# Fast-matrix feed-forward on one core: sums made in place of bank copies, loads issued by ScalarE

## The chip, the cores and the metric

The kernel runs on one core of one Trainium2 chip. The core has a matrix engine (TensorE, PE in the profile; its weight loads are PEld), VectorE (DVE), ScalarE (ACT), GpSimd (POOL) and SyncE (SP), which here only issues transfers. Each engine runs its own list of instructions in order, and the lists meet only through semaphores. A DMA is put into a queue by the engine that issues it, and 16 DMA engines carry it out. The metric is the device time of one execution in microseconds.

## The reference, cut to what matters

One encoder layer on 560 tokens (16 meta rows, 512 prompt frames, 32 frames of a running stream), width 2048, in float32:

```
xn   = RMSNorm(h);  P = xn @ w_in                      # q, k, v, gates, conv input
mix  = [stick-breaking attention heads | short gated conv groups], normed per group
h    = h + RMSNorm(mix @ w_out)
xf   = RMSNorm(h)
ff   = silu(xf @ w_gate) * (xf @ w_up)                 # D_FF = 5632
h    = h + RMSNorm(ff @ w_down)                        # the output; keys, values and conv rows go out too
```

The change touches only the feed-forward part, the last three lines, for the 544 tokens that are not meta rows.

## The kernel before, in words

Each float32 product is made of three: both operands are split into a rounded part and a rest (hi, lo), and hi*hi, hi*lo and lo*hi are summed in a PSUM bank. The feed-forward products use a scheme with 7 block products instead of 8: tokens are two halves of 272 (TH), inputs two halves of 8 blocks of 128 (KH), outputs two columns of 128. The seven products of a step are called B11, B21, T2, T3, T1, T4, B22, in this order; each is 24 matmuls of 128x128 by 272 columns. B11, B21 and B22 take a block of the weights as it is, T1 to T4 take combinations that VectorE makes (`combine`). The token side needs seven combinations too (A11, A12, S2, S3, S1, A22, S4).

There are 44 gate/up steps (even: gate, odd: up; a pair yields 256 columns of ff) and then 24 down steps (`DSTEPS`, in 6 blocks of 4 steps; a block takes 4, 4, 4, 4, 3, 3 pairs of ff, and its 4 steps cover the 2048 outputs). Step 43 is `LAST`, step 44 is the first down step (d = 0).

What each engine does in a step, in the order of its list:

- SyncE (L613 and on) loads the weights of the next step as two panels of 1 MB: `load_panel(step, 0)` once the seven tiles of the step before last are split, `load_panel(step, 1)` once tile T1 of the step before is split. Between the two stands, for even steps, `store_hidden`: it waits for `hid_split` and stores the seven combinations of a pair of ff (hid_hi and hid_lo, each 128 x 7 x 272 float32) to device memory. During the down steps its list also holds `load_hidden`, which brings a combination of a block of ff back into one of 12 slots (`xd`), two DMAs each. SyncE's queue is one list, so a wait for one transfer holds all behind it.
- ScalarE rounds each of the seven tiles (`tile_high`, L1336; tile i waits until product i-4 is done, as the ring has four places), copies bank snapshots after B11, T2 and T3 to m1, u2 and m7 (`copy_out`, L1369), applies silu to the quarters of the gate, and rounds the seven ff combinations (`round_hidden`, L1375).
- VectorE subtracts for each tile the rest (`tile_rest`, L1711), makes the combinations of the next step's weights (`combine`, L1725; T2 needs the second panel), adds bank and snapshot (`c11` L1778, `c22` L1784, `c21` L1789) into `gate` in gate steps and into `hid` in up steps, multiplies in place (`times_gate`, `times_gate_rest`), makes the four sums of ff (`hidden_sums`, in the gate step after) and the rest of the seven (`hidden_rest`, L1815, in the next up step), and in the down steps adds banks to y (`take_down`, L1874 and L1876).
- TensorE waits per product for its split tile and for the bank that it overwrites: B22 of a gate step for `c22_made`, T2 for `m1_copied`, T1 for `u2_copied`, T4 for `m7_copied`; in the down steps T2 waits for `take_down(B11)` of the same step.

The order of work is written out by hand; no planner sets it.

Of the kernel before, what the change touches and what calls it, by code (L numbers as in the profile page):

```python
# [25 lines left out]
P = 128  # L26
# [3 lines left out]
def build_layer(nc, x_prompt, x_sample, cache_k, cache_v, state_conv, meta, w_in, w_out, conv_w,  # L30
# [90 lines left out]
    with ExitStack() as ctx:  # L121
# [63 lines left out]
        m1 = sb_at("m1", 134144, [P, TH])  # L185
        u2 = sb_at("u2", 135232, [P, TH])
        m7 = sb_at("m7", 169984, [P, TH])
        t_hi = sb_at("t_hi", 137216, [P, RING_T, KH * P], F32R)
        t_lo = sb_at("t_lo", 153600, [P, RING_T, KH * P], F32R)
# [311 lines left out]
        def _(sp):  # L501
# [99 lines left out]
            def load_hidden(i):  # L601

                b, q = i // 7, i % 7
                sp.wait_ge(hid_stored, 32 * first_pair[b + 1])
                for part in range(2):
                    sp.dma_start(xd[:, i % XD, part, 0:KBS[b], :].bitcast(F32),  # L606
                                 ff_scr[part][:, HID_OF[q], first_pair[b]:first_pair[b + 1], :])\
                      .then_inc(xd_loaded[i % XD], 16)

            def load_hidden_after(step, q):  # L610

                if step == LAST and q < 6:
                    sp.wait_ge(product_done, 7 * step + q + 1)  # L613
                    load_hidden(2 * q)
                    load_hidden(2 * q + 1)
                elif step >= STEPS and (step - STEPS) % NQ == NQ - 1:
                    i = (step - STEPS) // NQ * 7 + q + XD
                    if i < 7 * len(KBS):
                        sp.wait_ge(product_done, 7 * step + q + 1)
                        load_hidden(i)  # L620

            for step in range(1, ALL):
                if step == 2:
                    sp.wait_ge(xs_lo, 8)
                if step > 2:
                    sp.wait_ge(tile_lo, 7 * (step - 1))
                if step == 1:
                    sp.wait_ge(tile_lo, T1 + 1)
                load_panel(step, 0)
                if step >= LAST + 2:  # L630
                    for q in range(4, 7):
                        load_hidden_after(step - 2, q)
# [421 lines left out]
        def _(act):  # L1054
# [310 lines left out]
            def copy_out(out, step, q, letter, made, free):  # L1365
                act.wait_ge(product_done, 7 * step + q + 1)
                if step:
                    act.wait_ge(free, step)
                A(out[:, :], step_bank(step, letter), ACT.Copy).then_inc(made, 1)  # L1369

            def round_hidden(j):
                act.wait_ge(hid_summed, 4 * (j + 1))
                if j:
                    act.wait_ge(hid_stored, 32 * j)
                nc.scalar.copy(hid_hi[:, :, :], hid[:, :, :]).then_inc(hid_rounded, 1)  # L1375

            for step in range(STEPS):
# [7 lines left out]
                copy_out(m1, step, B11, "a", m1_copied, c11_made)  # L1385
# [12 lines left out]
                tile_high(ahead)  # L1398
                tile_high(ahead + 1)
# [41 lines left out]
        def _(dve):  # L1441
# [326 lines left out]
            def quarters(step):  # L1768
                return hid if step % 2 else gate

            def c11(step):
# [4 lines left out]
                if step >= 3 and step % 2:  # L1776
                    dve.wait_ge(hid_stored, 32 * (step // 2))
                V.tensor_tensor(quarter(quarters(step), 0, 0), step_bank(step, "c"), m1[:, :], ALU.add)\  # L1778
                    .then_inc(c11_made, 1)

            def c22(step):
                dve.wait_ge(product_done, 7 * step + T1 + 1)
                dve.wait_ge(m7_copied, step + 1)
                V.tensor_tensor(quarter(quarters(step), 1, 1), step_bank(step, "a"), m7[:, :], ALU.add)                    .then_inc(c22_made, 1)  # L1784

            def c21(step):
                dve.wait_ge(product_done, 7 * step + T4 + 1)
                dve.wait_ge(u2_copied, step + 1)
                V.tensor_tensor(quarter(quarters(step), 1, 0), step_bank(step, "b"), u2[:, :], ALU.add)                    .then_inc(c21_made, 1)  # L1789

            def times_gate(step):
# [3 lines left out]
                V.tensor_tensor(quarter(hid, 0, 1), step_bank(step, "a"), quarter(gate, 0, 1), ALU.mult)                    .then_inc(c12_up, 1)  # L1795

            def times_gate_rest(step):
                dve.wait_ge(c21_made, step + 1)
                V.tensor_tensor(hid[:, 0:2, :], hid[:, 0:2, :], gate[:, 0:2, :], ALU.mult)
                V.tensor_tensor(hid[:, 3, :], hid[:, 3, :], gate[:, 3, :], ALU.mult).then_inc(hid_made, 1)  # L1800

            def hidden_sums(j):

                d21, d11, d12, d22, s1, s2, s4 = (hid[:, h, :] for h in range(7))
# [3 lines left out]
                V.tensor_tensor(d21, d11, d21, ALU.subtract).then_inc(hid_summed, 1)  # L1808
                V.tensor_tensor(s2, s1, d11, ALU.subtract).then_inc(hid_summed, 1)
# [8 lines left out]
            for step in range(STEPS):  # L1818
# [59 lines left out]
            for d in range(DSTEPS):  # L1878
# [9 lines left out]
                if d == 1:  # L1888
                    hidden_rest(FF // 2 - 1)
# [8 lines left out]
                if d == 0:  # L1898
                    hidden_sums(FF // 2 - 1)
# [125 lines left out]
```

## Time and profile before

| quantity | value |
|---|---|
| median of 3 runs | 2493.34 us (2493.3 to 2494.7) |
| the profiled execution: its own time | 2493.23 us |
| its span, first to last instruction | 2491.5 us, mean granted clock 0.981 |
| gate/up steps | from 972.2 to 1960.8 us |
| down steps | from 1960.8 to 2449 us |
| VectorE busy in the span | 1553.6 us |
| ScalarE busy in the span | 1009.2 us |

The span leaves 1.7 us outside. Busy time of TensorE counts a matmul from start to modelled end. A row of a timeline gives start and duration; in brackets stands how long the engine had been idle and what ended it.

### The profile page before, as it was taken

What the parts mean: (1) busy time and instruction counts of PE and PEld (TensorE: products, weight loads), DVE (VectorE), ACT (ScalarE), POOL (GpSimd) and SP (SyncE); (2) the same over time, 40 slices, a digit from 0 to 9 for tenths busy, and PEclk for the clock granted to TensorE, in tenths of its full rate; (3) what the DMA queues carried; (4) which work ended last, traced back from release to release, by engine and by line L of the source; (5) the groups of instructions that cost most, each with busy time, mean ns of one, the idle gap of its engine ahead of it and who ended that gap; (6) DMA issues with size and microseconds to landing.
All of it is one profiled execution on the core that took longest, in us unless ns stands there. A gap on an engine that the chain in (4) does not pass through costs nothing.

```text
span 2491.5 us, 42064 instructions
## 1 busy us (share of the span) xinstructions
PE 2382.3 (96%) x18188; PEld 2329.9 (94%) x18188; DVE 1553.6 (62%) x1755; ACT 1009.2 (41%) x1257; POOL 103.7 (4%) x155
## 2 busy tenths in 40 slices
PE   8999999999999994899999999999999889999996
PEld 7999999999999993899999999999999889999995
DVE  5324333343443228777777777777777678888896
ACT  6344444433333214544444444444444333333344
POOL 0000000000011110000000000000000000000024
PEclk9999999999999997899999999999999999999997
DMA  7222322232225321334454443445444845663552
GB/s 236 85 66 82 90 76 73 82 89 83 83 73 168 86 85 72 102 127 155 134 165 134 138 143 124 157 134 165 133 144 138 307 153 203 224 201 102 195 188 72
DMA packets 332636, 327.92 MB, mean 132 GB/s; under 512 B 8700, under 2 KB 291220, under 8 KB 332324
## 3 DMA queue, kind: packets, MB, share of 16 engines
q1 hardware_dynamic: 318080, 318.47, 40.0%
q10 hardware_dynamic: 14372, 6.77, 0.9%
q8 instruction: 144, 2.36, 0.4%
q14 instruction: 40, 0.33, 0.0%
HBM read 264.20 MB, written 61.00 MB: 131 GB/s over the span
## 4 chain that ended last, share of the span: by engine, by line
PE 80%; DVE 10%; issue 4%; ACT 4%; DMA 2%; SPq 1%; POOL 0%; POOLq 0%; ACTq 0%; DVEq 0%
PE ps L427 30%; PE ps L975 28%; PE ps L1032 17%; PE ps L742 4%; ACT t_hi L1336 2%; DVE t_lo L1711 2%; DVE panel L1725 2%; SPq L606 1%; DMA panel<-in_w_down_dram 1%; DMA ff_lo_scr<-hid_lo 1%; PE ps L686 1%; DVE xs L1733 1%; DVE misc L1737 0%; DVE y_left L1925 0%; DVE wide L1701 0%
## 5 line engine op out<-in xcount | busy, mean ns | idle before, releaser
L975 PE MATMUL ps<-xs,t_hi 128*128 128x272 f32 x4928 | 943.3, 291 | 51.0 <-DVE xs L1733 19.1
L975 PEld LDWEIGHTS ps<-xs,t_hi 128*128 128x128 f32 x4928 | 780.7, 190 | 57.2 <-issue 54.7
L975 PE MATMUL ps<-xs,t_lo 128*128 128x272 f32 x2464 | 716.6, 291 | 0.0
L1711 DVE TENSOR_TENSOR t_lo<-panel,t_hi 128x1024 fp32r<-128x1024 f32 (+1 forms) x405 | 485.9, 1200 | 195.1 <-ACT t_hi L1336 187.2
L1336 ACT CAST t_hi<-panel 128x1024 fp32r<-128x1024 f32 (+1 forms) x405 | 411.9, 1022 | 470.5 <-PE ps L1032 230.6
L1032 PE MATMUL ps<-xd,t_hi 128*128 128x272 f32 x2464 | 470.3, 290 | 16.9 <-DVE t_lo L1711 8.6
L975 PEld LDWEIGHTS ps<-xs,t_lo 128*128 128x128 f32 x2464 | 467.3, 190 | 0.0
L427 PE MATMUL ps<-act_hi,w_hi 128*128 128x272 f32 (+1 forms) x2048 | 435.6, 294 | 3.2 <-DVE act_lo L1548 2.1
L427 PE MATMUL ps<-act_lo,w_hi 128*128 128x272 f32 (+1 forms) x2048 | 427.0, 290 | 0.0
L427 PE MATMUL ps<-act_hi,w_lo 128*128 128x272 f32 (+1 forms) x2048 | 427.0, 290 | 0.0
L1032 PEld LDWEIGHTS ps<-xd,t_hi 128*128 128x128 f32 x2464 | 390.4, 190 | 18.7 <-issue 9.6
L1032 PE MATMUL ps<-xd,t_lo 128*128 128x272 f32 x1232 | 358.1, 291 | 0.0
L427 PEld LDWEIGHTS ps<-act_hi,w_hi 128*128 128x128 f32 x2048 | 323.0, 189 | 7.3 <-DVE act_lo L1548 2.5
L427 PEld LDWEIGHTS ps<-act_hi,w_lo 128*128 128x128 f32 x2048 | 324.3, 189 | 0.0
L427 PEld LDWEIGHTS ps<-act_lo,w_hi 128*128 128x128 f32 x2048 | 324.0, 189 | 0.0
L413 DVE TENSOR_TENSOR w_lo<-w_raw,w_hi 128x1024 fp32r<-128x1024 f32 x126 | 158.4, 1258 | 195.9 <-ACT w_hi L407 195.1
L407 ACT CAST w_hi<-w_raw 128x1024 fp32r<-128x1024 f32 x128 | 133.7, 1046 | 282.7 <-PE ps L427 222.5
L1032 PEld LDWEIGHTS ps<-xd,t_lo 128*128 128x128 f32 x1232 | 233.5, 190 | 0.0
L1336 ACT CAST t_hi<-t_raw 128x1024 fp32r<-128x1024 f32 (+1 forms) x68 | 69.8, 1026 | 64.1 <-PE ps L1032 35.7
L1725 DVE TENSOR_TENSOR t_raw<-panel,panel 128x1024 f32<-128x1024 f32 (+1 forms) x67 | 79.4, 1185 | 22.2 <-DMA panel<-in_w_down_dram 17.3
L1369 ACT ACTIVATE m<-ps 128x272 f32<-128x272 f32 x88 | 35.0, 398 | 142.2 <-PE ps L975 142.2
L1482 DVE TENSOR_TENSOR misc<-misc 128x1440 f32<-128x1440 f32 x8 | 13.3, 1658 | 114.3 <-ACT misc L1119 114.3
(176 smaller groups left out, 1746.0 us busy)
## 6 DMA issues: line engine op xcount, KB each, us to landing
w_raw<-in_w_in_dram SPq DMA_DIRECT2D x96, 512.0 KB, 3.9
panel<-in_w_up_dram SPq DMA_DIRECT2D x44, 1024.0 KB, 5.5
panel<-in_w_gate_dram SPq DMA_DIRECT2D x43, 1024.0 KB, 6.8
panel<-in_w_down_dram SPq DMA_DIRECT2D x32, 1024.0 KB, 6.5
ff_hi_scr<-hid_hi SPq DMA_DIRECT2D x22, 952.0 KB, 4.5
ff_lo_scr<-hid_lo SPq DMA_DIRECT2D x22, 952.0 KB, 7.6
w_raw<-in_w_out_dram SPq DMA_DIRECT2D x32, 512.0 KB, 4.1
xd<-ff_hi_scr SPq DMA_DIRECT2D x28, 544.0 KB, 9.4
```

The source lines that it names most:

```text
L407: nc.scalar.copy(w_hi[:, k % SLOTS, :], raw_slot(k)).then_inc(hi_ready, 1)
L413: engine.tensor_tensor(w_lo[:, k % SLOTS, :], raw_slot(k), w_hi[:, k % SLOTS, :].bitcast(F32), ALU.subtract).then_inc(lo_ready, 1)
L427: mm = nc.tensor.matmul(out[:, h, :], w[:, k, col:col + width], x[:, x_at + k, token + h * half:token + (h + 1) * half], start=begins, sto ...
L606: sp.dma_start(xd[:, i % XD, part, 0:KBS[b], :].bitcast(F32), ff_scr[part][:, HID_OF[q], first_pair[b]:first_pair[b + 1], :])\
L686: return nc.tensor.transpose(out, src, ident[0:n, 0:n])
L742: return nc.tensor.matmul(out, w, x, start=start, stop=True, skip_group_check=True)
L975: mm = nc.tensor.matmul(out, w[:, k, :], xs[:, x, part, k, :], start=begins and k == 0 and w is hi and part == 0, stop=k == KH - 1 and w i ...
L1032: mm = nc.tensor.matmul(out[:, n, :], w[:, k, n * P:(n + 1) * P], xd[:, slot, part, k, :], start=q in (B11, B21, T3) and k == 0 and w is h ...
L1336: nc.scalar.copy(tile_of(t_hi, i), raw_tile(i)).then_inc(tile_hi, 1)
L1369: A(out[:, :], step_bank(step, letter), ACT.Copy).then_inc(made, 1)
L1711: V.tensor_tensor(tile_of(t_lo, i), raw_tile(i), tile_of(t_hi, i).bitcast(F32), ALU.subtract)\
L1725: V.tensor_tensor(out, x, y, ALU.subtract).then_inc(t_made, 1)
```

## The change

The in-place results of the up step go: m1, u2 and m7 get a second buffer each, used in odd (up) steps, and c11, c22, c21 of an up step sum into them. The product with the gate then reads the buffer and the gate and writes `hid`. Around it the order of ff's sums, rounding and rest changes, and the loads of ff's combinations move from SyncE's list to ScalarE's; loads 7 to 11 of the start move from step 43/44 to step 45.

```diff
-        m1 = sb_at("m1", 134144, [P, TH])
-        u2 = sb_at("u2", 135232, [P, TH])
-        m7 = sb_at("m7", 169984, [P, TH])
+        m1, u2, m7 = ([sb_at(f"{name}_{odd}", (at, at_odd)[odd], [P, TH]) for odd in range(2)]
+                      for name, at, at_odd in (("m1", 134144, 171264), ("u2", 135232, 209024), ("m7", 170176, 136320)))
...
SyncE:
-                if step >= LAST + 2:
-                    for q in range(4, 7):
-                        load_hidden_after(step - 2, q)
                 if step > 3 and step % 2 == 0 and step // 2 - 2 < FF // 2:
                     store_hidden(step // 2 - 2)
-                if step >= LAST + 1:
-                    for q in range(2):
-                        load_hidden_after(step - 1, q)
...
-                if step >= LAST + 1:
-                    for q in range(2, 4):
-                        load_hidden_after(step - 1, q)
ScalarE:
-            def copy_out(out, step, q, letter, made, free):
+            def copy_out(out, step, q, letter, made):
                 act.wait_ge(product_done, 7 * step + q + 1)
-                if step:
-                    act.wait_ge(free, step)
-                A(out[:, :], step_bank(step, letter), ACT.Copy).then_inc(made, 1)
+                if step >= 2:
+                    if step % 2:
+                        act.wait_ge(hid_made, step // 2)
+                    else:
+                        act.wait_ge({B11: c11_made, T2: c21_made, T3: c22_made}[q], step - 1)
+                A(out[step % 2][:, :], step_bank(step, letter), ACT.Copy).then_inc(made, 1)
...
+            def load_hidden_after(step, q):
+                first = []
+                if step == LAST:
+                    first = {0: (0, 1), 1: (2, 3), 2: (4, 5), 3: (6,)}.get(q, ())
+                elif step == STEPS + 1 and 0 <= q < 5:
+                    first = (7 + q,)
+                for i in first:
+                    act.wait_ge(product_done, 7 * LAST + i // 2 + 1)
+                    load_hidden(i)
+                d = step - STEPS
+                if d >= 0 and d % NQ == NQ - 1 and 0 <= q < 7:
+                    i = d // NQ * 7 + q + XD
+                    if i < 7 * len(KBS):
+                        act.wait_ge(product_done, 7 * step + q + 1)
+                        load_hidden(i)
...
+                load_hidden_after(step, 0)
                 tile_high(7 * step + 5)
-                copy_out(u2, step, T2, "a", u2_copied, c21_made)
+                load_hidden_after(step, 1)
+                if not is_gate and j:
+                    round_hidden(j - 1)
+                copy_out(u2, step, T2, "a", u2_copied)
                 tile_high(7 * step + 6)
+                load_hidden_after(step, 2)
...
-                copy_out(m7, step, T3, "b", m7_copied, c22_made)
-                if is_gate and step:
-                    round_hidden(j - 1)
+                copy_out(m7, step, T3, "b", m7_copied)
                 tile_high(ahead)
+                load_hidden_after(step, 3)
...
-                    if d == 0 and q == 6:
+                    if d == 1 and q == 4:
                         round_hidden(FF // 2 - 1)
+                    if q == 3:
+                        load_hidden_after(STEPS + d - 1, 6)
+                    else:
+                        load_hidden_after(STEPS + d, q - 4)
VectorE:
+            def sum_of(step, up, t, n):
+                return up[1][:, :] if step % 2 else quarter(gate, t, n)
...
-                if step >= 3 and step % 2:
-                    dve.wait_ge(hid_stored, 32 * (step // 2))
-                V.tensor_tensor(quarter(quarters(step), 0, 0), step_bank(step, "c"), m1[:, :], ALU.add)\
+                V.tensor_tensor(sum_of(step, m1, 0, 0), step_bank(step, "c"), m1[step % 2][:, :], ALU.add)\
...
             def times_gate(step):
+                if step > 1:
+                    dve.wait_ge(hid_stored, 32 * (step // 2))
...
-                V.tensor_tensor(hid[:, 0:2, :], hid[:, 0:2, :], gate[:, 0:2, :], ALU.mult)
-                V.tensor_tensor(hid[:, 3, :], hid[:, 3, :], gate[:, 3, :], ALU.mult).then_inc(hid_made, 1)
+                V.tensor_tensor(quarter(hid, 0, 0), m1[1][:, :], quarter(gate, 0, 0), ALU.mult)
+                V.tensor_tensor(quarter(hid, 1, 1), m7[1][:, :], quarter(gate, 1, 1), ALU.mult)
+                V.tensor_tensor(quarter(hid, 1, 0), u2[1][:, :], quarter(gate, 1, 0), ALU.mult).then_inc(hid_made, 1)
...
                 if step % 2 and step > 1:
-                    hidden_rest(step // 2 - 1)
+                    hidden_sums(step // 2 - 1)
                 tile_rest(7 * step + 4)
+                if step % 2 and step > 1:
+                    more_hidden_sums(step // 2 - 1)
...
-                elif step % 2 == 0:
+                else:
                     c11(step)
+                if step % 2 and step > 1:
+                    hidden_rest(step // 2 - 1)
                 tile_rest(7 * step + 6)
...
-                if step % 2:
-                    c11(step)
-                if after_up:
-                    hidden_sums(step // 2 - 1)
                 tile_rest(ahead)
...
down steps:
                 if d == 1:
-                    hidden_rest(FF // 2 - 1)
+                    hidden_sums(FF // 2 - 1)
+                    more_hidden_sums(FF // 2 - 1)
...
                 tile_rest(7 * step + 6)
-                if d == 0:
-                    hidden_sums(FF // 2 - 1)
+                if d == 1:
+                    hidden_rest(FF // 2 - 1)
```

`more_hidden_sums` holds the last two of the four sums, `hidden_sums` the first two. `load_hidden` itself is unchanged but for its issuer.

## Rows read from the trace of the kernel before

**Rows 1.** The page, first part: busy time, share of the span, instructions.

```profile
PE 2382.3 (96%) x18188; PEld 2329.9 (94%) x18188; DVE 1553.6 (62%) x1755; ACT 1009.2 (41%) x1257; POOL 103.7 (4%) x155
```

**Rows 2.** Waits of TensorE, 1040 to 1950 us: total, times, longest.

```profile
PE ps L975 <- DVE gate L1784: 18.1, 21, 0.9
PE ps L975 <- DVE hid L1784: 0.8, 4, 0.2
```

**Rows 3.** Waits of TensorE, 1950 to 2400 us.

```profile
PE ps L1032 <- DVE t_lo L1711: 8.6, 2, 7.0
PE ps L1032 <- DVE y_left L1874: 6.6, 2, 5.3
PE ps L1032 <- DVE y_left L1876: 0.9, 1, 0.9
```

**Rows 4.** Timeline of TensorE: start, us, instruction [idle before <-released by].

```profile
1283.70 0.48 PE L975 MATMUL ps<-xs,t_hi 128*128 128x272 f32 x2 [0.86 <-DVE gate L1784]
...
1327.16 0.48 PE L975 MATMUL ps<-xs,t_hi 128*128 128x272 f32 x2 [0.86 <-DVE gate L1784]
...
1971.14 0.82 PE L1032 MATMUL ps<-xd,t_hi 128*128 128x272 f32 x2 [7.01 <-DVE t_lo L1711]
...
1977.23 0.48 PE L1032 MATMUL ps<-xd,t_hi 128*128 128x272 f32 x2 [1.26 <-DVE y_left L1874]
...
2006.90 0.79 PE L1032 MATMUL ps<-xd,t_hi 128*128 128x272 f32 x2 [5.30 <-DVE y_left L1874]
```

**Rows 5.** Timeline of VectorE in one pair of steps, and one later split.

```profile
1290.76 2.14 DVE L1815 TENSOR_TENSOR hid_lo<-hid,hid_hi 128x1904 fp32r<-128x1904 f32 x1
...
1305.35 1.22 DVE L1711 TENSOR_TENSOR t_lo<-panel,t_hi 128x1024 fp32r<-128x1024 f32 x1
...
1326.58 0.43 DVE L1784 TENSOR_TENSOR gate<-ps,m 128x272 f32<-128x272 f32 x1
...
1377.69 2.14 DVE L1815 TENSOR_TENSOR hid_lo<-hid,hid_hi 128x1904 fp32r<-128x1904 f32 x1
```

**Rows 6.** Timeline of ScalarE; the last line from its waits, 1020 to 1950 us.

```profile
1293.05 1.05 ACT L1336 CAST t_hi<-panel 128x1024 fp32r<-128x1024 f32 x1 [1.69 <-PE ps L975]
...
1304.17 1.06 ACT L1336 CAST t_hi<-panel 128x1024 fp32r<-128x1024 f32 x1 [3.73 <-DMA panel<-in_w_gate_dram]
...
1321.54 1.79 ACT L1375 CAST hid_hi<-hid 128x1904 fp32r<-128x1904 f32 x1 [0.86 <-DVE hid L1811]
...
1392.17 1.05 ACT L1336 CAST t_hi<-panel 128x1024 fp32r<-128x1024 f32 x1 [4.80 <-DMA panel<-in_w_gate_dram]
...
ACT t_hi L1336 <- DMA panel<-in_w_gate_dram: 68.6, 17, 5.0
```

**Rows 7.** Timeline of SyncE's issues (start, us of issuing).

```profile
1294.20 1.45 SPq L585 DMA_DIRECT2D panel<-in_w_gate_dram  x1
...
1948.63 1.24 SPq L606 DMA_DIRECT2D xd<-ff_lo_scr  x1
...
2049.22 0.43 SPq L606 DMA_DIRECT2D xd<-ff_lo_scr  x1
```

**Rows 8.** Timeline of VectorE in the first two down steps.

```profile
1968.72 1.23 DVE L1725 TENSOR_TENSOR t_raw<-panel,panel 128x1024 f32<-128x1024 f32 x1 [11.68 <-DMA panel<-in_w_down_dram]
...
1976.37 0.71 DVE L1874 COPY y_left<-ps 128x544 f32<-128x544 f32 x1
...
1995.90 1.22 DVE L1725 TENSOR_TENSOR t_raw<-panel,panel 128x1024 f32<-128x1024 f32 x1 [5.62 <-DMA panel<-in_w_down_dram]
...
2006.04 0.72 DVE L1874 COPY y_left<-ps 128x544 f32<-128x544 f32 x1
```

**Rows 9.** Windows of TensorE: length, busy, granted clock, DMA share, GB/s.

```profile
1296.00:1299.00 3.00, 3.00 (x26) 1.00 1.04 345
1971.00:1976.00 5.00, 4.82 (x24) 0.64 1.02 414
2006.90:2013.00 6.10, 6.10 (x30) 0.57 0.95 307
```

More of the change, by code:

```diff
@@ L184, in build_layer @@
         t2_raw = sb_at("t2_raw", 130048, [P, KH, P])
-        m1 = sb_at("m1", 134144, [P, TH])
-        u2 = sb_at("u2", 135232, [P, TH])
-        m7 = sb_at("m7", 169984, [P, TH])
-        t_hi = sb_at("t_hi", 137216, [P, RING_T, KH * P], F32R)
-        t_lo = sb_at("t_lo", 153600, [P, RING_T, KH * P], F32R)
+        m1, u2, m7 = ([sb_at(f"{name}_{odd}", (at, at_odd)[odd], [P, TH]) for odd in range(2)]
+                      for name, at, at_odd in (("m1", 134144, 171264), ("u2", 135232, 209024), ("m7", 170176, 136320)))
+        t_hi = sb_at("t_hi", 137408, [P, RING_T, KH * P], F32R)
+        t_lo = sb_at("t_lo", 153792, [P, RING_T, KH * P], F32R)
         h2_sq = sb_at("h2_sq", 35840, [P, KC, TL])
@@ L599, in store_hidden @@
                     sp.dma_start(ff_scr[part][:, :, j, :], src[:, :, :].bitcast(F32)).then_inc(hid_stored, 16)
[L601 to L620, printed above, removed]
             for step in range(1, ALL):
@@ L1375, in round_hidden, with load_hidden @@
                 nc.scalar.copy(hid_hi[:, :, :], hid[:, :, :]).then_inc(hid_rounded, 1)
+            def load_hidden(i):
+                b, q = i // 7, i % 7
+                act.wait_ge(hid_stored, 32 * first_pair[b + 1])
+                for part in range(2):
+                    act.dma_start(xd[:, i % XD, part, 0:KBS[b], :].bitcast(F32),
+                                  ff_scr[part][:, HID_OF[q], first_pair[b]:first_pair[b + 1], :])\
+                        .then_inc(xd_loaded[i % XD], 16)
+            def load_hidden_after(step, q):
[13 more added lines that the diff above has]
+                        load_hidden(i)
             for step in range(STEPS):
@@ L1384, in _ @@
                     x_high(S3, 0, 1, s_made, 2)
-                copy_out(m1, step, B11, "a", m1_copied, c11_made)
+                copy_out(m1, step, B11, "a", m1_copied)
                 tile_high(7 * step + 4)
@@ L1765, in _ @@
             x_rest(S2, 5, a11)
-            def quarters(step):
-                return hid if step % 2 else gate
+            def sum_of(step, up, t, n):
+                return up[1][:, :] if step % 2 else quarter(gate, t, n)
             def c11(step):
@@ L1783, in c22 @@
                 dve.wait_ge(m7_copied, step + 1)
-                V.tensor_tensor(quarter(quarters(step), 1, 1), step_bank(step, "a"), m7[:, :], ALU.add)                    .then_inc(c22_made, 1)
+                V.tensor_tensor(sum_of(step, m7, 1, 1), step_bank(step, "a"), m7[step % 2][:, :], ALU.add)\
+                    .then_inc(c22_made, 1)
             def c21(step):
@@ L1788, in c21 @@
                 dve.wait_ge(u2_copied, step + 1)
-                V.tensor_tensor(quarter(quarters(step), 1, 0), step_bank(step, "b"), u2[:, :], ALU.add)                    .then_inc(c21_made, 1)
+                V.tensor_tensor(sum_of(step, u2, 1, 0), step_bank(step, "b"), u2[step % 2][:, :], ALU.add)\
+                    .then_inc(c21_made, 1)
             def times_gate(step):
@@ L1794, in times_gate @@
                 dve.wait_ge(silu_made, 4 * (step // 2 + 1))
-                V.tensor_tensor(quarter(hid, 0, 1), step_bank(step, "a"), quarter(gate, 0, 1), ALU.mult)                    .then_inc(c12_up, 1)
+                if step > 1:
+                    dve.wait_ge(hid_stored, 32 * (step // 2))
+                V.tensor_tensor(quarter(hid, 0, 1), step_bank(step, "a"), quarter(gate, 0, 1), ALU.mult)\
+                    .then_inc(c12_up, 1)
             def times_gate_rest(step):
                 dve.wait_ge(c21_made, step + 1)
-                V.tensor_tensor(hid[:, 0:2, :], hid[:, 0:2, :], gate[:, 0:2, :], ALU.mult)
-                V.tensor_tensor(hid[:, 3, :], hid[:, 3, :], gate[:, 3, :], ALU.mult).then_inc(hid_made, 1)
+                V.tensor_tensor(quarter(hid, 0, 0), m1[1][:, :], quarter(gate, 0, 0), ALU.mult)
+                V.tensor_tensor(quarter(hid, 1, 1), m7[1][:, :], quarter(gate, 1, 1), ALU.mult)
+                V.tensor_tensor(quarter(hid, 1, 0), u2[1][:, :], quarter(gate, 1, 0), ALU.mult).then_inc(hid_made, 1)
+            d21, d11, d12, d22, s1, s2, s4 = (hid[:, h, :] for h in range(7))
             def hidden_sums(j):
-                d21, d11, d12, d22, s1, s2, s4 = (hid[:, h, :] for h in range(7))
                 dve.wait_ge(hid_made, j + 1)
@@ L1808, in hidden_sums, with more_hidden_sums @@
                 V.tensor_tensor(d21, d11, d21, ALU.subtract).then_inc(hid_summed, 1)
+            def more_hidden_sums(j):
                 V.tensor_tensor(s2, s1, d11, ALU.subtract).then_inc(hid_summed, 1)
```

## The prediction, made before the changed kernel was run

> **What bounds the kernel now.** The page's first part says that TensorE is busy for 2382.3 of 2491.5 us [rows 1], so only its gaps are to be won, plus what moves them. The waits of TensorE, read for the gate/up steps alone, show one kind of gap there: 21 times before product B22 of a gate step, 18.1 us in all, released by the sum at L1784, and four small ones before B22 of an up step, 0.8 us [rows 2]. The same view from 1950 us on shows the passage to the down products: waits for t_lo (8.6) and for y_left [rows 3]. All of these lie in steps 44 and 45; up to 2400 us there is no other. These two places are what the edits touch, so I walk each by its timeline.
>
> A clock for the walk: B22 of one gate step starts at 1283.70, that of the next at 1327.16 after a gap of 0.86 [rows 4]: (43.46 - 0.86) / 14 = 3.04 us a product, 21.3 a step. An up step starts at O = 1286.74; B21 of the gate step behind it is wanted at O + 8 x 3.04 = O + 24.34.
>
> **Gate/up steps, what goes.** In a gate step DVE makes hidden_sums ahead of tile_rest(ahead), ScalarE rounds hid (1.79 us at 1321.54) [rows 6] and casts the next tile after it; DVE waits for that cast, splits, combines, and only at 1326.58 + 0.43 is the sum done that B22 needs [rows 5]. With sums and rounding in the up step, the cast can start when product T3 is done (12.2 us after the gate step's start) and the copy made, and lasts from 12.6 to 13.6; split and combine (1.22 each, as at 1305.35 [rows 5]) end at 16.0, the sum at 16.5, and B22 is wanted at 18.3. The gap of 0.86 goes in all 21 gate steps. The up step's c11, whose wait for a store made its c22 late four times, no longer has that wait, so the 0.8 goes too: -18.9 us.
>
> **Gate/up steps, what comes late.** hidden_rest, which stood early in the up step and ended at 1290.76 + 2.14 = O + 6.16 [rows 5], now stands behind round_hidden, and that behind tile_high(+5). That cast starts at 1293.05 = O + 6.31, when B21 is done [rows 6]; + 1.0 + 1.79 for the rounding + 0.03 + 2.14 = O + 11.27. The three product-wise multiplications (0.1 us more than two) and the sums before it are done by O + 6.9, off the path. So the split of hid is 5.1 us later. SyncE waits for it in store_hidden and only then issues the second panel of the next gate step: the store goes out at the split's end, 1292.90, the panel at 1294.20 [rows 7], and it is first used at 1304.17, 11.27 us after the split's end [rows 6]. Store and panel stand in one queue and keep their order, so this distance stays: the panel lands at L = O + 22.5 instead of 17.4. From landing to B21's t_lo the old chain takes 1305.35 + 1.22 - 1304.17 = 2.40 (combine T2, then the split) [rows 5, 6], + 0.15 to TensorE: B21 starts at O + 25.1, wanted 24.3. Slack before: 4.4 us; now a gap of 0.72. The landing scatters: for the pair whose split starts at 1377.69 it is used 12.34 us after the split's end. ScalarE waited for such a panel 17 times, 68.6 us in all, 4.04 on average against the 3.73 at 1304.17, at most 5.0 [rows 5, 6]: the average distance is 0.3 to 0.4 longer than 11.27, and the mean gap 1.1 us. It falls on the gate steps 4 to 42, 20 times: +22.4 us. Bounds: all at 11.3, 20 x 0.7 = 14; all at the longest wait's 12.5, 20 x 2.0 = 39. Behind the gap nothing more is late by my walk: copy m1, which T2 waits for, is made at L + 5.35 and T2 wants it at L + 5.6, a margin of 0.2 that I count as zero and up to +2 us in all.
>
> Balance of this stage: -18.9 + 22.4 = +3.5 (from -5 to +20).
>
> **The passage, step 43 to 44.** With the last up step at O' = 1971.14 - 7.01 - 24.34 = 1939.79 [rows 4], the second panel of step 44 lands at 1968.72 = O' + 28.9 [rows 8], behind a store and eight loads of hid. T2 of step 44 starts 8.5 us after that landing (take_down ends 1976.37 + 0.71, TensorE 1977.23 [rows 4, 8]) where it was wanted at O' + 27.4: 10.1 us lost, of it 7.01 and 1.26 as gaps [rows 4] and the rest at half clock: from 1971 to 1976 the granted clock is 0.64 of 2.4 GHz [rows 9], that is 1.2 GHz for most of it, after seven idle us. Now ScalarE issues loads 0 to 6 (one issue took 0.43 on SyncE [rows 7], so 0.8 a pair, 5.6 us of ScalarE in a step in which its casts wait for TensorE, 1.69 us at 1293.05 [rows 6]): two pairs before tile_high(+5), hence hid's split ends at O' + 13.1 and not 11.3. At O' + 14.4, when the store's data start, the loads have moved 3.4 of their 7.8 MB (7 x 2 x 128 x 4352 B) at 0.41 MB/us [rows 9]; the other 4.4 MB take 10.7 us. Store and panel, 3.0 MB, take 8.3 us at 0.345 to 0.38 (the first is the rate of 1296 to 1299 us, a store [rows 9]). If the panel's queue is served first it lands at O' + 24.4 (13.1 + 11.3), if last at 14.4 + 19 = 33.4; equal shares of bytes would give 14.4 + 2 x 3.0 / 0.4 = 29.4. No row shows two busy queues. I take 31.5, since loads move in pieces of 4352 B and stores in 1088 B. Cost 31.5 + 8.5 - 27.4 = 12.6 against 10.1: +2.5 (bounds -4.6 to +4.4).
>
> The Trainium skill ("DMA: Bandwidth & Descriptors", Issuing engines are not separate DMA queues, and Arbitration) says that queues of different issuers run on the same 16 engines and take turns packet by packet. By that rule the panel neither passes nor waits for all loads, L = 29.4 to 33.4; the trace of before can't bear it out, and it speaks against a gain from issuing on ScalarE.
>
> **Steps 44 to 46.** Before, four more pairs of loads stood ahead of the second panel of step 45: landed 1995.90 [rows 8], gaps 0.9, 1.6 (the rest of the 8.6) and 5.30 [rows 3, 4] and then 0.57 of the full clock over 6.1 us [rows 9], 2.6 us lost: 10.4 in all. These loads now come in step 45, and the rounding too: the panel of 45 is in time, -10.4. But in step 45 the split of hid moves behind tile_rest(+6): T2 done 9.1, cast to 10.2, split to 11.4, hidden_rest to 13.5 (before 2006.04 with PE held up by the gap). Its store, a pair of loads (2.7 us) and the second panel of step 46 follow: landing 13.5 + 11.3 + 2.7 = 27.5 to 27.9 (24.8 at least, 29 at most). From landing to take_down(B11), for which T2 waits, the old chain is 2006.04 + 0.72 - 1995.90 less the 2.06 of hidden_rest in it = 8.8, + 0.15 [rows 8]. T2 of 46 starts at 36.8, wanted 27.4: +9.4 (6.4 to 10.5). Balance of both: 2.5 - 10.4 + 9.4 = +1.5 (-8.6 to +4.5).
>
> **Elsewhere.** In the later down steps a pair of loads costs ScalarE 0.8 us per product of 3.04, less than the 1.69 that a cast waits; the panels there no longer stand behind SyncE's loads, and share the engines with them: both hidden now, no gap shown before, counted 0. Ramp (steps 0, 1) and tail: same order, 0.
>
> **Sum.** 2493.2 (profiled execution; the median is 2493.3) + 3.5 + 1.5 = 2498.2 us. What a measurement can tell from no change is 0.2%, 5 us: the forecast lies on that bound.
>
> **Rivals.** (A) The forecast: the panel of the gate steps late by about 1.1 us: chance 0.50, own range 2491 to 2505. (B) Late landings become the rule (12.3 and more, with copy m1 late besides): +36 - 18.9 + 1.5 = 2512; for it, waits of up to 5.0 in rows 6; against it, that the same transfers follow each other as before. 0.17. (C) Faster, at the passage: the panels, no longer behind eight loads in their own queue, are served as if alone: -8.6 + 3.5 = 2488; it decides from a landing before O' + 27. For it, that they leave the queue in which they waited; against it, that the bytes ahead are the same. 0.13. (D) Faster, in the gate/up steps: the panel lands by O + 21.8, because the distance of 11.3 shrinks by 0.7; then the gap is nil: -18.9 + 1.5 = 2476. Against it, that the mean wait lies above the 3.73 and not below. 0.10. (E) Slower, the issuing engine: ScalarE's issues take 1.24 us each, as one of SyncE's right behind a store [rows 7], not 0.43; the 14 issues of step 43 then take 17 us instead of 6, and copies and casts come late by up to 11 less some 3 of slack, +8: 2506. 0.10.
>
> Slower by over 0.2%: half of A less a little, B, E: 0.48. Within: 0.28. Faster: C, D and an edge of A: 0.24. Range, from C to B: 2485 to 2511.
>
> **What would show it.** Right: no gap before B22 of gate steps; instead a gap of 0.7 to 2 us before B21 of every gate step from 4 on, released by t_lo, with ScalarE's wait for panel<-in_w_gate grown from 3.7 to about 8.8 us; hidden_rest ending at O + 11.3; T2 of step 44 and of step 46 held by y_left, step 45 clean. Wrong: if the panel's wait on ScalarE stays at 4 us, the shift by SyncE's order is wrong; if step 44's landing is before O' + 27, the queues' shares are; a gap in a later down step would mean that loads and panels collide.

## The result and the profile after

The changed kernel takes 2504.25 us (median of 17 runs, 2496.49 to 2507.24) against 2493.78 us (17 runs, 2491.52 to 2494.94): ratio 1.0038, interval 1.0031 to 1.0046. It is slower by 10.5 us by the medians. The profiled execution took 2504.82 us (span 2503.1, granted clock 0.978) against 2493.23: +11.6, where the prediction had +5.0.

The page's first part for the changed kernel, answering to [rows 1]:

```profile
PE 2387.0 (95%) x18188; PEld 2335.1 (93%) x18188; DVE 1550.3 (62%) x1777; ACT 998.9 (40%) x1257; POOL 103.7 (4%) x155
```

The matmuls are the same in number and 4.7 us longer in sum. So no work was added; the windows below show stretches at the low clock, which fit the difference. Waits of TensorE (total, times, longest), first 1040 to 1950 us, then 1950 to 2400 us, answering to [rows 2, 3]:

```profile
PE ps L944 <- DVE t_lo L1721: 22.0, 20, 2.0
...
PE ps L1001 <- DVE t_lo L1721: 19.4, 2, 11.6
PE ps L1001 <- DVE y_right L1892: 0.7, 1, 0.7
PE ps L1001 <- DVE y_left L1892: 0.6, 1, 0.6
```

The 21 gaps before B22 are gone, and 20 gaps before B21, on the split of its tile, stand in their place. ScalarE's wait for the second panel shows what they come from; its line in [rows 6] had 68.6 us in 17 waits:

```profile
ACT t_hi L1305 <- DMA panel<-in_w_gate_dram: 189.5, 20, 10.4
```

9.5 us on average. One pair of steps, VectorE and then ScalarE: the split of hid ends at 1294.20, the panel is used 12.1 us later, and TensorE's gap follows (first line of the third fence). The later lines are from the passage: step 44's second panel is used at 1979.55, and the split of step 45 at 2014.86 is followed by the use of step 46's panel at 2033.07.

```profile
1292.06 2.14 DVE L1833 TENSOR_TENSOR hid_lo<-hid,hid_hi 128x1904 fp32r<-128x1904 f32 x1
...
1979.55 1.23 DVE L1735 TENSOR_TENSOR t_raw<-panel,panel 128x1024 f32<-128x1024 f32 x1 [17.21 <-DMA panel<-in_w_down_dram]
...
2014.86 2.13 DVE L1833 TENSOR_TENSOR hid_lo<-hid,hid_hi 128x1904 fp32r<-128x1904 f32 x1
...
2033.07 1.23 DVE L1735 TENSOR_TENSOR t_raw<-panel,panel 128x1024 f32<-128x1024 f32 x1 [12.54 <-DMA panel<-in_w_down_dram]
```

```profile
1290.25 1.78 ACT L1349 CAST hid_hi<-hid 128x1904 fp32r<-128x1904 f32 x1
...
1306.28 1.05 ACT L1305 CAST t_hi<-panel 128x1024 fp32r<-128x1024 f32 x1 [9.60 <-DMA panel<-in_w_gate_dram]
```

```profile
1308.64 0.52 PE L944 MATMUL ps<-xs,t_hi 128*128 128x272 f32 x2 [1.23 <-DVE t_lo L1721]
...
1485.73 0.52 PE L944 MATMUL ps<-xs,t_hi 128*128 128x272 f32 x2 [1.99 <-DVE t_lo L1721]
...
1617.40 0.52 PE L944 MATMUL ps<-xs,t_hi 128*128 128x272 f32 x2 [1.99 <-DVE t_lo L1721]
...
1662.00 0.52 PE L944 MATMUL ps<-xs,t_hi 128*128 128x272 f32 x2 [0.45 <-DVE t_lo L1721]
...
1981.96 0.82 PE L1001 MATMUL ps<-xd,t_hi 128*128 128x272 f32 x2 [11.63 <-DVE t_lo L1721]
...
2035.49 0.82 PE L1001 MATMUL ps<-xd,t_hi 128*128 128x272 f32 x2 [7.75 <-DVE t_lo L1721]
```

Two of the gaps in the gate steps are 1.99 us long. Behind the one the clock stays up, behind the other it falls (windows of TensorE: length, busy, granted clock, DMA share, GB/s):

```profile
1485.73:1489.33 3.60, 3.60 (x28) 1.00 0.00 0
1617.40:1621.00 3.60, 3.60 (x19) 0.63 0.00 0
```

This happens three times, behind gaps of 1.99, 1.96 and 1.96 us, and costs 1.5 us each: from 1617.40 to 1662.00, less the gap of 0.45, it is 44.15 us, and 42.63 to 42.65 in the periods that stay at the full clock.

Last, the passage. The DMA queues of the changed kernel at 1964 to 1968 us and at 1972 to 1976 us; q1 is SyncE's (store, then panel), q10 ScalarE's (loads of ff); columns are packets, MB and share of the 16 engines:

```profile
q10 hardware_dynamic: 329, 1.29, 79.0%
q1 hardware_dynamic: 327, 0.36, 24.5%
...
q1 hardware_dynamic: 1157, 1.37, 100.6%
q10 hardware_dynamic: 40, 0.10, 6.5%
```

Both queues move as many pieces, but a load's piece has 4352 B and a store's 1088 B: the store gets 22% of the bytes until the loads run dry.

**Where the 11.6 us come from.** From the B21 of one gate step to that of the next it is 42.37 us where no gap is (first experiment). In the changed kernel it is 42.64 plus the gap, whatever the gap's length (0.39 to 1.99 us): each costs 0.27 us beyond its length. Before, with a gap of 0.86, it was 43.46 [rows 4]: 0.23 beyond. So the gate/up steps gave back 18.9 us of gaps and 5.8 beyond them (25 gaps of 0.23 or 0.24), and took 22.0, 5.4 beyond them (20 x 0.27) and 4.5 at half clock: +7.2. The passage cost +5.8: T2 of step 44 starts 14.7 us late (10.1 before), step 45 has no gap (-10.4), T2 of step 46 starts 11.2 late, 0.4 at low clock besides. What stands before step 4 is 0.7 shorter and the tail 0.3; 0.4 is unaccounted.

### The profile page after: what moved, and what is told of

Read it like the earlier page. It is cut to its first block, busy times and chain, and to the rows that moved or that the text cites. A ratio compares the mean times of both kernels' runs of the same rounds, so it can differ in the third digit from the quotient of the medians.

```text
span 2503.1 us, 42089 instructions
## 1 busy us (share of the span) xinstructions
PE 2387.0 (95%) x18188; PEld 2335.1 (93%) x18188; DVE 1550.3 (62%) x1777; ACT 998.9 (40%) x1257; POOL 103.7 (4%) x155
## 3 DMA queue, kind: packets, MB, share of 16 engines
q8 instruction: 144, 2.36, 0.4%
## 4 chain that ended last, share of the span: by engine, by line
PE 74%; DMA 10%; DVE 9%; ACT 3%; issue 2%; SPq 1%; POOL 0%; ACTq 0%; DVEq 0%; POOLq 0%
PE ps L426 30%; PE ps L944 22%; PE ps L1001 17%; DMA panel<-in_w_gate_dram 8%; PE ps L711 4%; DVE hid_lo L1833 2%; DMA panel<-in_w_down_dram 1%; DVE t_lo L1721 1%; ACT hid_hi L1349 1%; DVE t_raw L1735 1%; SPq L598 1%; DVE xs L1743 1%; PE ps L655 1%; DVE panel L1735 0%; DVE misc L1747 0%
## 5 line engine op out<-in xcount | busy, mean ns | idle before, releaser
L1001 PE MATMUL ps<-xd,t_hi 128*128 128x272 f32 x2464 | 471.3, 291 | 21.4 <-DVE t_lo L1721 19.4
L1735 DVE TENSOR_TENSOR panel<-panel 128x1024 f32<-128x1024 f32 (+1 forms) x68 | 83.0, 1221 | 0.0
```

The costliest lines, as they stand in the source:

```text
L1001: mm = nc.tensor.matmul(out[:, n, :], w[:, k, n * P:(n + 1) * P], xd[:, slot, part, k, :], start=q in (B11, B21, T3) and k == 0 and w is h ...
L1735: V.tensor_tensor(out, x, y, ALU.subtract).then_inc(t_made, 1)
```

## The experiments

Each kernel has 4 or 5 runs (e2_passage 11) beside runs of the kernel before, whose medians are 2493.4 to 2493.8. "After" is the changed kernel. One execution of each was profiled.

**1. e1_gate: in the gate/up steps the panel ahead of the store.** In SyncE's loop:

```diff
-                if step > 3 and step % 2 == 0 and step // 2 - 2 < FF // 2:
+                if step > 3 and step % 2 == 0 and step // 2 - 2 < FF // 2 and not (step < STEPS):
                     store_hidden(step // 2 - 2)
...
                 load_panel(step, 1)
+                if step > 3 and step % 2 == 0 and step // 2 - 2 < FF // 2 and (step < STEPS):
+                    store_hidden(step // 2 - 2)
```

> The changed kernel, with one edit in SyncE's list for the steps before 44: the second panel is issued ahead of the store of ff's combinations, not behind it. Theory (order): the panel of a gate step is late only because it stands behind a store that now waits for the later split. With it ahead, all 20 gaps before B21 go (22.0 us in the profile) and the three stretches at half clock behind them (1.5 each); the passage to the down steps keeps its 26 us: about 2504 - 26 = 2478 us. Rival 1 (VectorE): the gap is the late combine and split on VectorE, whose up step is now fuller; then gaps stay near 1 us and the time near 2504. Rival 2 (bytes): store and panel share the engines in any order, gaps shrink to half, 2490.

Measured: 2472.89 us (2470.99 to 2473.84), ratio 0.9917 [0.9903, 0.9930]; 31.4 below after. TensorE has no wait at all from 1040 to 1940 us. Two neighbouring splits of hid on VectorE are shown; the 18 distances between 1117.11 and 1879.83 are 42.36 to 42.39 us, 42.37 on average:

```profile
1837.45 2.15 DVE L1835 TENSOR_TENSOR hid_lo<-hid,hid_hi 128x1904 fp32r<-128x1904 f32 x1
1879.83 2.14 DVE L1835 TENSOR_TENSOR hid_lo<-hid,hid_hi 128x1904 fp32r<-128x1904 f32 x1
```

The passage keeps its waits (first two of its lines):

```profile
PE ps L1003 <- DVE t_lo L1723: 18.2, 2, 11.8
PE ps L1003 <- DVE y_left L1894: 1.2, 1, 1.2
```

So the panel's place behind the store is the whole cause of the 20 gaps. The gain in these steps is 22.0 + 4.5 + 20 x 0.27 = 31.9 by the numbers above; the forecast left out what a gap costs beyond its length. (Between the two profiled executions it is 33.8; step 46 has 1.4 of the rest, a gap of 6.40 where after has 7.75.)

**2. e2_passage: the same exchange for `step >= STEPS` alone.**

> The changed kernel, with the same edit only from step 44 on. Theory (order): the second panels of steps 44 and 46 land in time, the 14.7 and 11.6 us lost there go, the gate steps keep their gaps: 2504 - 26 = 2478 us. Rival (shares): the panel of step 44 still has the loads of ScalarE's queue beside it from the 4th us on, lands some 10 us before the end of the step and costs nothing, or, if the loads are served first, lands at 26 us after the step's start and costs 7: 2485. Rival (bytes): the delay only moves to a later transfer, 2495.

Measured: 2493.23 us (2489.03 to 2496.33), ratio 0.9994 [0.9985, 1.0003]: 11.0 below after, not 26. A miss. Waits from 1950 us on:

```profile
PE ps L1003 <- DVE y_left L1894: 8.4, 1, 8.4
PE ps L1003 <- DVE y_right L1894: 4.8, 1, 4.8
```

The waits for t_lo are gone: the panels are in time. But now the store is late, and `times_gate` of step 43 (7.5 us) and `take_down` of step 46 (2.6 us) wait for it (`hid_stored`). That is the last rival of the expectation, with its 2495 us. The late transfer has changed its name, not gone.

**3. e3_both: both exchanges.**

> The changed kernel with the second panel ahead of the store in all steps. If the two places are independent, as the theory has it, their gains add: 2504 - 26 - 26 = 2452 us, under the kernel before by 1.7%. If the store, now later still, holds something new (VectorE's times_gate waits for it; the next panel stands behind it), some of it comes back: 2465.

Measured: 2465.23 us (2463.99 to 2467.04), ratio 0.9886 [0.9872, 0.9899]. The second case of the expectation. VectorE's `times_gate` in step 43 shows who waits for the store, and the queues at 1932 to 1936 us show why it is late:

```profile
1947.53 0.44 DVE L1810 TENSOR_TENSOR hid<-ps,gate 128x272 f32<-128x272 f32 x1 [7.03 <-DMA ff_lo_scr<-hid_lo]
```

```profile
q10 hardware_dynamic: 331, 1.29, 78.5%
q1 hardware_dynamic: 331, 0.36, 24.9%
```

**4. e4_before_gate: the first exchange in the kernel before.** Is the order alone to thank, without the new buffers?

> The kernel before, with the second panel ahead of the store in the steps before 44. There the panel lands 4.4 us before it is needed, so the order is worth nothing: 2493.5 within 2 us, the 21 gaps of 0.86 before B22 unchanged. If the order by itself were a gain (rival: store and panel collide in any schedule), it would show here as 5 us or more.

Measured: 2631.53 us (2629.62 to 2635.5), ratio 1.0554 [1.0540, 1.0569]. A complete miss, by 138 us. In four fences: the waits of VectorE over 1040 to 1950 us in the kernel before and in this one, those of TensorE in this one, and a window of this one behind such a gap:

```profile
DVE hid L1778 <- DMA ff_lo_scr<-hid_lo: 45.1, 17, 3.4
```

```profile
DVE hid L1780 <- DMA ff_lo_scr<-hid_lo: 143.6, 18, 8.9
```

```profile
PE ps L977 <- DVE hid L1786: 79.9, 17, 5.7
```

```profile
1292.81:1299.61 6.80, 6.80 (x33) 0.56 0.00 0
```

There c11 of the up step sums into `hid`, which the store still reads. With the store behind the panel, c11 waits 8 us on average, B22 of the up step 4.1 to 5.7, and a stretch at half clock follows, 6.8 us long in the case shown. With the separate buffers no such wait is left (e1_gate). By themselves they bought 0.8 us of gaps; what they allow is the exchange: -31 us with them, +138 without. The two kernels also differ in the order of the sums and the split, so the part of the buffers is read from the waits; no run has the buffers alone.

**5. e5_loads_sp: after, with the loads of ff back in SyncE's list at the old places.**

```diff
+                if step >= LAST + 1:
+                    for q in range(2):
+                        load_hidden_after(step - 1, q)
...
             def load_hidden_after(step, q):      # ScalarE's
+                pass
```

> The changed kernel with the loads of ff's combinations back in SyncE's list, at the places and steps that they had before; all else as changed. What the move to ScalarE is worth. Theory (bytes ahead): in step 44 the panel stands behind the same store and four pairs of loads in one queue, landing some 32 us after step 43's start, 13 us lost (14.7 with ScalarE's queue); in step 45 the 10 us of the kernel before come back; in step 46 the panel stands behind the store alone, 6.4 lost and not 11.6. Sum 30 against 26: 2508 us. Rival: ScalarE's issues themselves cost time in its list; then the gate steps or step 43 get faster and the time is below 2500.

Measured: 2508.83 us (2506.54 to 2510.98), ratio 1.0060 [1.0048, 1.0073], as expected. It is 4.6 us above after by the medians; the runs overlap (lowest here 2506.54, highest of after 2507.24). That is the worth of the whole move, issuer and places together: loads 7 to 11 also go back from step 45 to steps 43 and 44. The profiles place it at the passage: from the start of step 43 to T2 of step 46 it takes 102.4 us here and 96.0 in after. Waits from 1950 us on, which after has as 19.4, 0.6 and 0.7:

```profile
PE ps L1031 <- DVE t_lo L1726: 17.9, 3, 10.5
PE ps L1031 <- DVE y_left L1897: 4.2, 2, 3.4
PE ps L1031 <- DVE y_right L1897: 1.9, 1, 1.9
PE ps L1031 <- issue: 1.3, 1, 1.3
```

**6. e10_more_store: after, with hid_hi stored a second time, to memory that nobody reads.** Three megabytes before the panel instead of two.

```diff
-                for part, src in enumerate((hid_hi, hid_lo)):
+                for part, src in enumerate((hid_hi, hid_lo, hid_hi)):
```

> The changed kernel with a third part in each store: hid_hi is stored once more, into a scratch tensor that nothing reads. The suspected cost is so increased by half, all else is as changed. Theory (the panel stands behind the store's bytes): distance from the split's end to the panel's first use 11.3 to 12.8 now 14.1 to 15.6 (0.975 MB at 0.352 MB/us = 2.8 us), gap before B21 1.1 to 3.9 on average, 20 times, +55 us; +6 at the passage. On the clock: gaps to 1.6 us never had a half-clock stretch behind them, those of 1.9 to 2.0 had one in 3 of 4 cases, those over 4 always; so nearly each of these gaps should now have one of 3.4 to 6.8 us, 1.7 us or more lost each, +30. Sum 2595 us. Rival (clock not moved by gaps under 4 us): 2562. Rival (the store hides in SyncE's slack): below 2520.

Measured: 2587.98 us (2585.58 to 2588.52), ratio 1.0375 [1.0361, 1.0389]. TensorE's waits over 1040 to 1950 us, and the clock behind a gap of 4.06 us:

```profile
PE ps L944 <- DVE t_lo L1721: 68.1, 18, 4.5
```

```profile
1623.90:1627.30 3.40, 3.40 (x17) 0.58 0.00 0
```

All 20 gaps together are 75.2 us, 77 were expected: the wait grows as the bytes ahead of the panel. The stretches at half clock behind them cost some 27 us (each period less its gap, against 42.64), a few less than expected; the time is 7 us below the 2595 forecast.

**7. e8_layout: after, with ff stored as (P, FF//2, 7, TH).** A store's row is then 7616 B in one piece, a load's piece 1088 B: the shares should turn round.

```diff
-        ff_scr = [nc.dram_tensor(f"ff_{part}_scr", (P, 7, FF // 2, TH), F32, kind="Internal").ap()
+        ff_scr = [nc.dram_tensor(f"ff_{part}_scr", (P, FF // 2, 7, TH), F32, kind="Internal").ap()
```

> The changed kernel with another layout of the scratch tensor in device memory: the store writes pieces of 7 x 1088 bytes, the loads read pieces of 1088 instead of 4352. Nothing else is changed. Theory (queues alternate piece by piece, rates by piece size 0.35 and 0.41 MB/us): store 0.8 us shorter, mean gap before B21 of the gate steps 1.1 to 0.4, half clock gone: -18; at the passage the store and the panel get the larger part, the panel lands some 10 us earlier: -12. 2474 us. Rival (queues share bytes evenly, whatever the piece): only the first part, 2486. Rival (loads of small pieces bind the down steps): new gaps there, 2500 or more.

Measured: 2480.07 us (2476.9 to 2484.72), ratio 0.9946 [0.9933, 0.9958]. Queues at 1944 to 1948 us; TensorE's waits for t_lo in the gate steps; ScalarE's first late copy in step 43, and the issue before it:

```profile
q1 hardware_dynamic: 320, 1.16, 75.6%
q10 hardware_dynamic: 323, 0.35, 25.5%
```

```profile
PE ps L944 <- DVE t_lo L1721: 4.9, 8, 0.9
```

```profile
1937.38 4.23 ACTq L1356 DMA_DIRECT2D xd<-ff_lo_scr  x1
...
1941.99 0.40 ACT L1343 ACTIVATE m<-ps 128x272 f32<-128x272 f32 x1 [5.86 <-issue]
```

Equal pieces again, and now q1 has the bytes. In this window q1 carries the store's end and the start of the panel, 3.6 kB a piece on average; from 1941 to 1944 us, with the store alone, it is 159 pieces against 160 and 1.09 MB against 0.16. Step 44's panel lands 15.3 us after the split (1937.07 to 1952.32), in after 21.4 (1958.17 to 1979.55). The store in long pieces is quicker alone too: the gaps of the gate steps fall from 22.0 to 4.9 us. The price: with many small pieces queued, one issue holds ScalarE for 4 us and more, and TensorE waits 3.9 us for that copy. So the passage gave 4 us and not the 12 expected (start of step 43 to T2 of step 46: 91.8 against 96.0), the gate steps more than the 18 expected, and the time lies between the theory (2474) and the rival (2486).

**8. Towards a better kernel, all with both exchanges of e3_both.** e6_later_loads issues loads 7 to 11 a step later (`step == STEPS + 2`). e7_spread_loads also issues load 4 after tile 3 of step 43, load 5 after its last tile and load 6 in step 44; e9_spread_more issues 5 and 6 one product later still. e11_spread_layout is e9 with the layout of e8; e12_one_a_tile is e11 with one load per tile in step 43:

```diff
-                    first = {0: (0, 1), 1: (2, 3), 2: (4, 5), 3: (6,)}.get(q, ())
+                    first = {0: (0,), 1: (1,), 2: (2,), 3: (3,), 6: (4,)}.get(q, ())
+                elif step == STEPS and q in (0, 1):
+                    first = (5 + q,)
```

> The kernel with the second panel ahead of the store in all steps (2465.2 us), with one more edit: loads 7 to 11 in step 46 and not in step 45. There T2 of step 46 waited 5.0 us for a take_down that waits for the store, and 3.4 us ran at half clock behind it. Theory (the store shares the engines with these loads and gets the smaller part): the gap and the half clock go, -6.5: 2459 us. Rival: the store is late by its own split (13.6 us into step 45) and the panel ahead of it; then nothing changes.

> The same, and in addition load 4 after the first tile of step 44 is cast, loads 5 and 6 at the start of step 44, so that only four pairs are ahead of the store in step 43. Theory: while both queues hold work the store of 1088-byte pieces gets a fifth of the bytes beside loads of 4352-byte pieces; with fewer loads beside it, it lands by 26 us after step 43's start, where times_gate wants it at 27. The 8.1 us before T2 of step 44 and the half clock behind them (10.2 us, 4 to 5 lost) go but for 1 us: 2448 us. Rival (latency): the store's landing is bound by its split, gap of 5 or more: 2456. Rival: a late load stops TensorE in step 44 instead.

> The kernel at 2457.0 us (second panel ahead of the store, loads spread), with loads 5 and 6 one product later each. In its profile T2 of step 44 waits 6.4 us for a take_down behind times_gate, which waits 5.3 us for the store of hid_lo; loads 5 and 6 are issued just when that store is under way. Theory (the queues alternate piece by piece, so any load beside the store takes four fifths): without them the store lands some 3 us sooner, the gap is 3 and the half clock behind it may go: 2452 us. Rival (the store is bound by its split and its own 5.5 us): no change, 2457.

> The first kernel of this call with the layout in which the store writes pieces of 7 x 1088 bytes and the loads read pieces of 1088. Theory: beside loads of small pieces the store takes most of the bytes, lands by 23 us after step 43's start, and T2 of step 44 waits for nothing: 2446 us. But in the profile with this layout alone ScalarE stood 5.9 us at its issues in step 43 (four times the pieces), and TensorE 3.9 for copy m7; if that stays, 2452; if the later loads bind the down steps, 2460.

> The kernel at 2453.6 us (panel first, spread loads, small pieces for the loads), with one load after each tile of step 43 and not two (load 4 at the start of step 44). In its profile ScalarE's fourth load took 4.35 us to issue and the next ones 1.5 each, copy u2 came late, TensorE stood 3.7 us in step 43 and ran 3.4 us at half clock. Theory (an issue stalls when a queue holds too many pieces, not for its place): both go, -5: 2448 us. Rival: the issues stall all the same, since one load of small pieces takes 3.1 us and one comes each 3.0 us: 2453.

| kernel | median (us) | lowest, highest | ratio to before |
|---|---|---|---|
| e6 | 2457.68 | 2456.57, 2460.99 | 0.9858 [0.9845, 0.9872] |
| e7 | 2457.01 | 2456.39, 2458.25 | 0.9854 [0.9839, 0.9869] |
| e9 | 2454.85 | 2451.0, 2456.41 | 0.9840 [0.9825, 0.9852] |
| e11 | 2453.60 | 2452.51, 2454.76 | 0.9838 [0.9825, 0.9852] |
| e12 | 2454.81 | 2450.98, 2456.74 | 0.9840 [0.9826, 0.9853] |

e6 did what was expected: the wait for y_right, 5.0 us, went. e7 missed: the one gap left shrank from 7.8 to 6.4 us only (in e9 to 5.3):

```profile
PE ps L1003 <- DVE y_left L1896: 6.4, 1, 6.4
```

With the layout (e11, e12) it is gone, and ScalarE's issues have taken its place: in e11 an issue of 4.35 us in step 43 and behind it a wait of TensorE for a copy (two fences), in e12 an issue of 6.75 us (the third).

```profile
1922.97 4.35 ACTq L1358 DMA_DIRECT2D xd<-ff_hi_scr  x1
```

```profile
PE ps L946 <- ACT u L1345: 3.7, 1, 3.7
```

```profile
1930.37 6.75 ACTq L1358 DMA_DIRECT2D xd<-ff_lo_scr  x1
```

e9 came between its two cases (2452 and 2457), e11 and e12 at the cases in which the stall stays (2452 and 2453). e9, e11 and e12 can't be told apart. They take some 39 us less than before and 50 less than after.

## Why the prediction was right, and where its sizes were off

The sign and the mechanism were right, and the time lies in its range, 6 us above its value; the profiled execution came out at +11.6 and not +5.0. The sign was no strong call: the prediction gave 0.48 to being slower by over 0.2%. Its range of 2485 to 2511 does not end at its own C and B (2488 and 2512), which changes nothing here.

- **What goes.** As forecast: no gap before B22. Its price was 18.9 us of gaps; their worth was some 25 (21 x 1.09, and 4 x 0.24 + 0.8), and what took their place is undervalued in the same way.
- **What comes late.** The split of hid ends at 1294.20, and O is 1308.64 - 1.23 - 24.34 = 1283.07: O + 11.1, forecast 11.27. The gaps are 22.0 us in 20, forecast 22.4 in 20. That closeness is partly luck: the panel is used 11.96 us after the split's end on average, where 11.6 to 11.7 was forecast (+0.3 a gap), and from O to the split and from the panel's use to B21 it is 0.3 us shorter than in the walk (11.1 for 11.27, 2.36 for 2.55). Either alone would have moved the sum by 6 us. The prediction named a gap of 0.7 to 2 us in every gate step as the sign of being right; 11 of the 20 are so, nine are 0.4 to 0.6. ScalarE's mean wait is 9.5, forecast 8.8. e1_gate and e10_more_store show the cause by taking it away and by enlarging it.
- **The term that is missing: the clock.** The walk counted a gap as its length. Three of the 20 brought 1.5 us each at half clock, 4.5 us. The trace of before showed half clock behind the 7.01 and 5.30 of the passage; that gaps near 2 us would bring it was not weighed.
- **Step 44.** The mis-sized term is the landing. O' is 1981.96 - 11.63 - 24.34 = 1945.99, the landing at O' + 33.6; taken was 31.5, the upper bound was 33.4. It lies above that bound although the split ended at O' + 12.2 and not 13.1. The bounds were not built alike: the first (24.4) gives store and panel 10.0 us from O' + 14.4 on, 1.7 more than the 8.3 of their bytes, and the last leaves the 1.7 out; with it the last is 35.1. And the walk let the store's data start 1.3 us after the split. Beside the loads the store, issued at 1958.20, moves its first piece after 1962.0, 3.9 us later and at O' + 16.1; alone, in a gate step, it is 1.0 us (issued at 1294.23, first piece after 1295.2). SyncE's issue, and both queues from 1962.0 to 1962.5 us:

```profile
1958.20 0.52 SPq L598 DMA_DIRECT2D ff_hi_scr<-hid_hi  x1
...
q10 hardware_dynamic: 45, 0.17, 91.5%
q1 hardware_dynamic: 27, 0.03, 16.2%
```

  Equal shares of bytes, and any value between the bounds, were weighed without knowing what is shared: the queues move equal numbers of pieces, so that the store got 22% of the bytes, nearly the "served last" case. The prediction did lean that way for the right reason, the sizes of the pieces.
- **Step 45** is clean, as forecast (-10.4). **Step 46**: the split ends at O + 13.6 (forecast 13.5), the panel lands at O + 29.7 (forecast 27.5 to 27.9, at most 29). Behind the split the loads still moved 1.8 MB, where the walk had one pair, 1.1 MB, and the store, issued at 2017.02, moved nothing before 2021.0. T2 is 11.2 us late, forecast 9.4; its last wait is y_right, 0.7 us, not y_left. The passage together is +5.8, forecast +1.5.
- **Rivals.** C needed a landing before O' + 27 in step 44, and there was none. D needed the distance of 11.3 to shrink: it ran from 11.25 to 12.85. For B, 6 of the 20 are 12.3 or more, and copy m1 was not late. E is out: the 14 issues of step 43 took 0.33 to 0.74 us each, the first of them beside a cast:

```profile
1949.33 0.36 ACTq L1356 DMA_DIRECT2D xd<-ff_hi_scr  x1
1949.48 1.04 ACT L1305 CAST t_hi<-panel 128x1024 fp32r<-128x1024 f32 x1
1949.71 0.46 ACTq L1356 DMA_DIRECT2D xd<-ff_lo_scr  x1
```

- **The rule of the Trainium skill** ("DMA: Bandwidth & Descriptors", Queues, rings and completion order, under Arbitration) says that an engine takes turns between the queues packet by packet. The traces agree with the turns: 329 pieces against 327, 320 against 323; how many pieces make a turn they don't show. The same page's section Issuing engines are not separate DMA queues says that starting DMAs on several engines saves only the time of issuing. The move was worth 4.6 us (e5_loads_sp), but it also changed which transfers stand before which and when five of the loads go out, so this run neither bears the sentence out nor contradicts it; which part of the 4.6 is issue time is open.

Open: why the distance from the split to the panel's use is now 11.3, now 12.1 and more; why a store waits 3.9 us for its first piece while loads are queued; and what decides that one gap of 1.99 us brings half clock and the next does not.

## What to carry to other kernels

When a step is moved later, look for what is issued behind its result: here a store that nobody needed soon held a panel that everybody needed, and one exchange of two lines was worth three times what the whole change had cost. Before such an exchange, find every reader and writer of the stored buffer: a buffer of its own may show no gain and yet decide the sign of the next step (-31 or +138 us). Where two queues are busy at once, count pieces, not bytes, to see who is served.

## What the runs showed of the hardware

- Two busy queues move equal numbers of pieces (329 and 327 in 4 us), so bytes go by the size of a piece: 78% to 4352 B against 1088 B; with the sizes turned round (7616 B against 1088 B, e8_layout), 1.09 MB to 0.16 in 3 us, by 159 pieces and 160.
- A store issued beside a queue full of loads moves its first piece 3.9 us after its issue (after, 1958.20) or 4.0 (2017.02), and in 1.0 us where no other queue is busy (1294.23).
- Half clock follows some of TensorE's gaps and not others of the same length: behind none of 15 gaps of 0.4 to 1.6 us, behind 3 of 5 between 1.86 and 1.99 (after); behind 3 of 8 near 3.1 us and 12 of 12 from 4.0 us on (e10_more_store). The changed kernel's runs scatter by 10.8 us, those of the one before by 3.4; that these stretches are the reason is likely and not shown, as one run was profiled: of the 17 runs the longest (2507.24 us) has a granted clock of 0.977, the shortest (2496.49) 0.980.
- A gap of TensorE costs 0.23 to 0.27 us more than its length in the profile, and no more for 1.99 us than for 0.39 (periods less their gap of 42.63 to 42.65 us in after, 42.60 before, against 42.37 with none in e1_gate).
- ScalarE's issue of a DMA runs beside its own cast (1949.33 and 1949.48), but takes 4 to 7 us when many pieces of 1088 B are queued (4.23 in e8_layout, 4.35 in e11, 6.75 in e12), and what stands behind it in ScalarE's list waits.
